# A two-layer diffusion backbone on one core: attention items scored two ahead in two row halves, and the differential head's maps subtracted before they are turned

## The reference

```python
qa,ka,va, qb,kb,vb, cq,ckv,kpe, qd,kd,vd = split(h @ w_in)       # h: norm(x), modulated by adaLN
oa = sdpa(qa, ka, va, sink)                                      # A: windowed, 4 heads, sink logit
ob = rmsnorm(softmax(q1 k1) @ vb - lam * softmax(q2 k2) @ vb)    # B: differential, 4 heads of two maps
oc = sdpa(up(norm(cq)), [up(norm(ckv)), rope(kpe)], v_mla)       # C: latent attention, rank-compressed
od = sdpa(qd, kd, vd, bias)                                      # D: neighbourhood, bias and mask
x += gate * norm(concat(oa, ob, oc, od) @ w_o)
x += gate * norm(ffn(h))      # layer 0: dense SwiGLU; layer 1: top-2 of 8 SwiGLU experts with a router
```

## Time and profile before

| what | us |
|---|---|
| median of 3 runs | 1674.35 (1673.54 to 1676.71) |
| profiled execution | 1674.89 |
| its span, first to last instruction | 1673.1 |
| attention loop, layer 0 (first scores to the first matmul of the projection) | 105.89 to 175.54 |
| the same, layer 1 | 498.01 to 568.65 |
| layer 1, last residual of the mixer to the first gather | 602.85 to 642.0 |
| experts' loop | 642.0 to 1655 |

### The profile page before, as it was taken

One profiled execution on the slowest core, in us unless ns is written; L12 is line 12 of the kernel. 1 busy time (PEld: TensorE's weight loads), 2 busy tenths in 40 slices (PEclk: granted clock), 3 DMA queues, 4 the chain that ended last, 5 costly groups with the idle time before them and its releaser, 6 DMA issues.

```text
span 1673.1 us, 22863 instructions
## 1 busy us (share of the span) xinstructions
PE 1576.5 (94%) x8167; PEld 1295.3 (77%) x8167; DVE 1194.3 (71%) x1014; ACT 976.9 (58%) x958; POOL 89.1 (5%) x142
## 2 busy tenths in 40 slices
PE   5998899999989868999999999999999999999996
PEld 2866789988777747888888888888888888888885
DVE  2556444534556425888888888888888888888885
ACT  4343444434534344776776776776776776776773
POOL 2410040000020010000000000000000000000001
PEclk8999899999989778999999999999999999999998
DMA  9864484577634344998998998998998998998991
GB/s 370 274 195 150 165 257 153 186 240 280 236 117 152 126 152 146 367 368 321 360 371 321 359 369 320 362 365 323 363 363 321 363 365 321 364 365 320 365 366 50
DMA packets 218291, 473.87 MB, mean 283 GB/s; under 512 B 8464, under 2 KB 41536, under 8 KB 218240
## 3 DMA queue, kind: packets, MB, share of 16 engines
q1 hardware_dynamic: 215024, 466.38, 78.3%
q0 software_dynamic: 3216, 6.79, 1.6%
HBM read 470.62 MB, written 2.52 MB: 283 GB/s over the span
## 4 chain that ended last, share of the span: by engine, by line
PE 89%; DVE 4%; ACT 2%; DMA 2%; issue 1%; POOL 1%; POOLq 0%; SPq 0%; DVEq 0%; ACTq 0%
PE ps L1541 22%; PE ps L1546 22%; PE ps L1542 22%; PE ps L1556 3%; PE ps L1557 3%; PE ps L1563 3%; PE ps L1922 2%; PE ps L1751 2%; DMA raw<-in_w_ada 2%; PE ps L1934 1%; PE ps L1715 1%; PE ps L1586 1%; PE ps L1625 1%; DVE w_lo L1060 1%; PE ps L1597 1%
## 5 line engine op out<-in xcount | busy, mean ns | idle before, releaser
L1060 DVE TENSOR_TENSOR w_lo<-raw,w_hi 128x2048 fp32r<-128x2048 f32 (+1 forms) x397 | 903.4, 2284 | 204.7 <-ACT w_hi L712 203.6
L712 ACT ACTIVATE w_hi<-raw 128x2048 fp32r<-128x2048 f32 (+1 forms) x397 | 757.5, 1913 | 254.0 <-PE ps L1542 237.1
L1541 PE MATMUL ps<-w_hi,x_hi 128*128 128x512 f32 (+1 forms) x1216 | 435.2, 370 | 6.5 <-ACT w_hi L712 2.7
L1542 PE MATMUL ps<-w_hi,x_lo 128*128 128x512 f32 (+1 forms) x1216 | 426.7, 363 | 0.0
L1546 PE MATMUL ps<-w_lo,x_hi 128*128 128x512 f32 (+1 forms) x1216 | 284.4, 364 | 0.0
L1541 PEld LDWEIGHTS ps<-w_hi,x_hi 128*128 128x128 f32 x1216 | 228.8, 188 | 47.1 <-issue 7.8
L1542 PEld LDWEIGHTS ps<-w_hi,x_lo 128*128 128x128 f32 x1216 | 228.8, 188 | 36.1
L1546 PEld LDWEIGHTS ps<-w_lo,x_hi 128*128 128x128 f32 x1216 | 206.6, 188 | 39.6
L1541 PE MATMUL ps<-w_hi,h_hi 128*128 128x512 f32 x528 | 207.8, 394 | 0.0
L1542 PE MATMUL ps<-w_hi,h_lo 128*128 128x512 f32 x528 | 207.4, 393 | 0.0
L1546 PE MATMUL ps<-w_lo,h_hi 128*128 128x512 f32 x528 | 141.2, 392 | 0.0
(11 more groups left out here) (242 smaller groups left out, 1213.1 us busy)
## 6 DMA issues: line engine op xcount, KB each, us to landing
raw<-in_moe_w_gate SPq DMA_DIRECT2D x112, 1024.0 KB, 5.2
raw<-in_moe_w_up SPq DMA_DIRECT2D x112, 1024.0 KB, 5.3
raw<-in_moe_w_down SPq DMA_DIRECT2D x112, 1024.0 KB, 5.2
raw<-in_w_ada SPq DMA_DIRECT2D x48, 1024.0 KB, 5.4
raw<-in_w_in SPq DMA_DIRECT2D x20, 960.0 KB, 11.6
raw<-in_ffn_w_gate SPq DMA_DIRECT2D x11, 1024.0 KB, 5.4
raw<-in_ffn_w_up SPq DMA_DIRECT2D x11, 1024.0 KB, 6.4
raw<-in_ffn_w_down SPq DMA_DIRECT2D x11, 1024.0 KB, 5.2
```

Of the source, the lines that this page charges most:

```text
L712: act.activation(split_hi(c, slice(0, width(c))), raw[:, r % NRAW, 0:width(c)], ACT.Copy).then_inc(hi_done, 1)
L1060: dve.tensor_sub(split_lo(c, n), raw[:, raw_of(c) % NRAW, n], split_hi(c, n)).then_inc(lo_done, 1)
L1541: pe.matmul(out, xh, split_hi(c, w), start=start, stop=False, skip_group_check=True)
L1542: last = pe.matmul(out, xl, split_hi(c, w), start=False, stop=False, skip_group_check=True)
```

## The change

Four things change. (1) Items are scored two ahead rather than one; `probs` gets four buffers (on the memory of `x_hi` and `x_lo`, which are free then). (2) For s = 1 the scores use only the 64 rows in which a head's queries aren't zero, alternating between the two halves of the array, which write two PSUM banks; heads of C and D are stored in the order 0, 2, 1, 3. (3) In B0 and B1 DVE's `soft_diff(i + 1)` subtracts the second map, scaled, from the first, so that two maps are turned, copied and multiplied with the values, where there were four. (4) Orders are moved: C5 before C3 and C4; `ada` 20 and 21 into items 8 and 9 (and before the last `w_o` units in the stream); `w_o` units split in items 6, 8 and 9; `out_T` of stream 0 into banks 0 and 1, without its wait for the fifth modulation row; the router's load behind item 9's output; and in layer 1, ACT copies the last modulation row and splits the second expert unit ahead of `norm_sq(1, 1, 1)`.

```diff
-LATER = ["C2", "C3", "C4", "C5"]
+LATER = ["C2", "C5", "C3", "C4"]
...
-        units += ada(l, 12, 13, 14, 15, 16, 17) + wo[:1] + ada(l, 18) + wo[1:2] + ada(l, 19) + wo[2:]
+        units += ada(l, 12, 13, 14, 15, 16, 17) + wo[:1] + ada(l, 18) + wo[1:2] + ada(l, 19, 20, 21) + wo[2:]
...
-        probs = nc.alloc_sbuf_tensor_at("probs", [P, 2, 4, 256], F32, offset=x_hi_at)
+        probs_all = nc.alloc_sbuf_tensor_at("probs", [P, 2, 2, 4, 256], F32, offset=x_hi_at)
...
-            return ps[:, 6:8, :] if s == 0 else ps[:, 4:6, :]
+            return ps[:, 4 * s:4 * s + 2, :]
...
+                if l:
+                    pool.wait_ge(o_evac, 20)
+                    pool.dma_start(rtr, router[0].rearrange("(k p) e -> p k e", p=P)).then_inc(in_rtr, 16)
...
-            pool.wait_ge(x_upd, 6)
-            pool.dma_start(rtr, router[0].rearrange("(k p) e -> p k e", p=P)).then_inc(in_rtr, 16)
...
# ACT, the attention loop
+                for i in range(2):
+                    exps(l, i)
                 for i in range(10):
-                    if i in (4, 8):
-                        rows(l, 2 + i // 4)
-                    exps(l, i)
                     if i in (0, 2, 4, 6):
                         prep(l, len(FIRST[0]) + i // 2)
-                    if i in (6, 8):
-                        split_to(wo_u(l, 0) + i // 2 - 2)
+                    if i + 2 < 10:
+                        exps(l, i + 2)
+                    if i in (3, 7):
+                        rows(l, 3 + i // 4)
+                    if i >= 6:
+                        split_to(wo_u(l, 0) + {6: 1, 7: 1, 8: 2, 9: 3}[i])
...
                 norm_h(l, 1, 0)
                 if l == 0:
                     norm_hi(l, 1, 0)
+                else:
+                    rows(l, 5)
+                    split_to(wo_u(l, 2) + 2)
                 norm_sq(l, 1, 1)
-                if l:
-                    rows(l, 5)
...
# DVE
+            def soft_diff(l, i):
+                s = i % 2
+                nk = nk_of(s)
+                dve.wait_ge(o_evac, 10 * l + i - 1)
+                dve.wait_ge(probs_ready, 10 * l + i + 1)
+                link(dve.reciprocal(sm[:, s, 20:24], sm[:, s, 8:12]))
+                link(dve.scalar_tensor_tensor(out=sm[:, s, 24:26], in0=sm[:, s, 8:12:2], scalar=lam[:, 4:5], in1=sm[:, s, 21:24:2],
+                                              op0=ALU.mult, op1=ALU.mult))
+                for h in range(2):
+                    last = dve.scalar_tensor_tensor(out=probs(i)[:, 2 * h, 0:nk], in0=probs(i)[:, 2 * h + 1, 0:nk],
+                                                    scalar=sm[:, s, 24 + h:25 + h], in1=probs(i)[:, 2 * h, 0:nk],
+                                                    op0=ALU.mult, op1=ALU.add)
+                last.then_inc(diff_ready, 1)
...
                 soft_pre(l, 0)
+                soft_pre(l, 1)
                 for i in range(10):
-                    if i + 1 < 10:
-                        soft_pre(l, i + 1)
                     soft_T(l, i)
+                    if i + 1 < 10 and ITEMS[(i + 1) // 2] in ("B0", "B1"):
+                        soft_diff(l, i + 1)
+                    if i + 2 < 10:
+                        soft_pre(l, i + 2)
                     if i in (1, 3, 5, 7):
                         prep(l, len(FIRST[1]) + i // 2)
...
-                    if i in (6, 8):
-                        split_to(wo_u(l, 0) + i // 2 - 2)
+                    if i >= 6:
+                        split_to(wo_u(l, 0) + {6: 1, 7: 1, 8: 2, 9: 3}[i])
...
# PE
+                def rows(n):
+                    return slice(64 * (n // 2), 64 * (n // 2) + 64) if s else slice(0, P)
+
+                for group in ((0, 2), (1, 3)) if s else ((0,), (1,), (2,), (3,)):
+                    for n in group:
+                        h = head_at(it, n)
+                        m = 2 * (h % 2) + h // 2 if it == "A" else h
+                        k = nk * (KEYS[it] + (h // 2 if it in ("C", "D") else 0))
+                        last = pe.matmul(v[:, n, :], qz[rows(n), QZ[it], s, m, :], keys[s][rows(n), k:k + nk], start=True, stop=it != "C")
...
                 item_scores(l, 0)
+                item_scores(l, 1)
                 for i in range(10):
-                    if i + 1 < 10:
-                        item_scores(l, i + 1)
                     item_T(l, i)
+                    if i + 2 < 10:
+                        item_scores(l, i + 2)
                     if i < 8:
                         prep(l, i % 2, len(FIRST[i % 2]) + i // 2)
-                        ada(l, 12 + i)
+                    ada(l, 12 + i)
...
-                pe.wait_ge(row_evac, SECTIONS.index((l, 4)) + 1)
...
-                ada(l, 20)
+                ada(l, 22)
                 norm_T(l, 1, 0)
-                for n in (21, 22, 23):
-                    ada(l, n)
+                ada(l, 23)
```

More of the change, by code:

```diff
@@ L790, in exps @@
                 for h in range(4):
-                    src = probs[:, s, h, 0:nk] if biased else score_view(s)[:, h, :]
-                    last = act.activation(probs[:, s, h, 0:nk], src, ACT.Exp, bias=sm[:, s, 4 + h:5 + h],
+                    src = probs(i)[:, h, 0:nk] if biased else score_view(s)[:, h, :]
+                    last = act.activation(probs(i)[:, h, 0:nk], src, ACT.Exp, bias=sm[:, s, 4 + h:5 + h],
                                           scale=1.0 if biased else SCALE[it], accum_out=sm[:, s, 8 + h:9 + h])
@@ L1181, in soft_pre @@
                 if it == "D" and s == 1:
-                    pv = probs[:, 1, :, :]
-                    dve.scalar_tensor_tensor(out=pv[:, :, 0:P], in0=v[:, :, 0:P], scalar=sc,
-                                             in1=bm.rearrange("p (h k) -> p h k", h=4), op0=ALU.mult, op1=ALU.add)
+                    pv = probs(i)
+                    for a in range(2):
+                        dve.scalar_tensor_tensor(out=pv[:, 2 * a:2 * a + 2, 0:P], in0=v[:, 2 * a:2 * a + 2, 0:P], scalar=sc,
+                                                 in1=bm.rearrange("p (b a k) -> p a b k", b=2, a=2)[:, a], op0=ALU.mult, op1=ALU.add)
                     link(dve.tensor_scalar(pv[:, :, P:2 * P], v[:, :, P:2 * P], sc, None, ALU.mult))
@@ L1710, in item_scores @@
                 if i >= 8:
-                    pe.wait_ge(prep_evac[s], np_(s) * (l + 1))
-                for h in range(4):
-                    m = 2 * (h % 2) + h // 2 if it == "A" else h
-                    k = nk * (KEYS[it] + (h // 2 if it in ("C", "D") else 0))
-                    last = pe.matmul(v[:, h, :], qz[:, QZ[it], s, m, :], keys[s][:, k:k + nk], start=True, stop=it != "C")
+                    pe.wait_ge(prep_evac[s], np_(s) * (l + 1) - 1)
+                def rows(n):
[6 more added lines that the diff above has]
+                        last = pe.matmul(v[:, n, :], qz[rows(n), QZ[it], s, m, :], keys[s][rows(n), k:k + nk], start=True, stop=it != "C")
                     if it == "C":
                         k = nk * KEYS["rope"]
-                        last = pe.matmul(v[:, h, :], qz[:, QZ["rope"], s, h, :], keys[s][:, k:k + nk], start=False, stop=True)
+                        for n in group:
+                            last = pe.matmul(v[:, n, :], qz[rows(n), QZ["rope"], s, n, :], keys[s][rows(n), k:k + nk], start=False, stop=True)
                 last.then_inc(scores, 1)
@@ L1728, in item_T @@
                 for kb in range(1 + i % 2):
-                    for h in range(4):
-                        last = pe.transpose(ps[:, kb, cols(h, P)], probs[:, i % 2, h, cols(kb, P)], ident())
+                    for h in range(2 if pairs else 4):
+                        last = pe.transpose(ps[:, kb, cols(h, P)], probs(i)[:, 2 * h if pairs else h, cols(kb, P)], ident())
                 last.then_inc(pT, 1)
@@ L1734, in item_out @@
                 it, s = ITEMS[i // 2], i % 2
-                n = 10 * l + i
-                pe.wait_ge(pt_evac, n + 1)
-                if n:
-                    pe.wait_ge(o_evac, n)
-                for h in range(4):
+                if it == "C":
+                    pe.wait_ge(prep_evac[s], np_(s) * (l + 1))
+                pe.wait_ge(pt_evac, 10 * l + i + 1)
+                if l or i:
+                    pe.wait_ge(o_evac, 10 * l + i)
+                for n in range(2 if it in ("B0", "B1") else 4):
+                    h = head_at(it, n)
                     if it == "A":
```

52 lines of the change are left out of this document (31 added, 21 removed).

## The result

The kernel before takes 1673.94 us (median, 1673.44 to 1676.71). The changed kernel takes **1646.45 us** (four runs: 1641.05, 1646.1, 1646.8, 1648.74), a ratio of 0.9828 with a 95% interval of 0.9801 to 0.9854. The forecast of 1641 is 5.5 us low; the time lies in its range, and the change is faster. Its profiled execution is the one of 1641.05, with a span of 1639.2 for 1673.1: 33.9 us less, where the sum of the prediction said 33.2. It is the fastest of the four.

A forecast was written before the change was run, and what follows sets the result against it. The unchanged experts' loop, 1005 of 1673.1 us, passes on whatever is gained ahead of it. Attention's 15.2 plus 18.0 behind layer 1's mixer make 33.2, taking 1674.89 to 1641.7, median 1641; range 1633 to 1655.

The forecast's parts named there:

- The order decides: Attention loops: new order followed queue to queue gives 62.0 for 69.65 us, 7.6 us a layer, 15.2 for both.
- the stretch that was counted as DVE's: Attention loop, from T1's copy to the end of soft_pre(8): DVE has no gap, 26.3 us.
- Row halves: Attention scores of s = 1: 5.0 us a layer off PE; with no overlap the path is 0.7 us a layer longer.
- scores, both halves at once, 0.95: Attention: s = 1 scores take 0.95 us in place of 1.78 with both array halves working at once.
- the prediction's own estimate with ten changes: Attention: ten more tiling changes a layer, up to 0.15 us each, leave 3.5 of the row halves' 5.0 us.
- Halved maps: Attention, B0 and B1: two maps for four halve transposes and outputs, 4.2 us a layer off PE; DVE isn't relieved.
- The tail: Behind layer 1's mixer: earlier router load and ACT's new order start the top-2 choice earlier, 18.0 us gained.
- the gates at full clock: Behind layer 1's mixer: gates take 1.8 us, for 3.58 at half clock, ending at 610.9.
- The prediction's own bound for half clock: Behind layer 1's mixer: with PE at half clock throughout, gates and logits end at 616.6, a gain of 16.8 us.
- I leave the 3.2 in: Attention: old order counted 66.4 for the trace's 69.65; these 3.2 us, mostly PE's half-speed tail, stay in the new count.
- The rival of the kept clock: Attention loops' ends and projection: PE keeps its clock, so the gain is 45 us, 1630; chance 0.07.
- DVE holding everything up: Attention, B items: soft_diff waits for late exponentials with DVE's queue behind it; gain only 21 us, 1653; chance 0.17.

The follow-up runs named there:

- four maps with full rows: Changed kernel with both row halves and subtracted maps undone, scoring two ahead and moved orders kept: 1648.92 us, ratio 0.9845.
- four maps alone: Changed kernel without soft_diff, four maps turned, copied and multiplied again in B0 and B1, row halves kept: 1651.96 us, ratio 0.9863.
- both versions: Changed kernel with 14, 8 and 24 matmuls feeding nothing: 1643.31 us; changed kernel with full rows, 8 and 18 such matmuls, memsets moved: 1638.95 us.
- the filled kernel: Changed kernel plus identity matmuls feeding nothing: 14 after out_T(0) per layer, 8 before stream 1's norm, 24 before the first gather: 1643.31 us.
- the early load with ACT's new order: Kernel before with the early router load, and modulation row and second expert unit ahead of stream 1's sum of squares: 1660.97 us, ratio 0.9921.
- the late load: Changed kernel with the router's load back at its old place: 1658.32 us, ratio 0.989.

## Why the prediction held, point by point

The sum's agreement with the profiled execution (33.9 for 33.2) is in part luck: attention gave 1.9 us more than forecast and the start 1.2 that nobody forecast, the tail 0.9 less, and two stretches between them lost 1.5.

- **The order decides**: right, and shown. Attention fell by 17.1 us for both layers in the profiled execution, where 15.2 were forecast. One item ahead costs 14.0 of it. The wait that it leaves in front of the projection, 3.1 us, came out to the tenth, and the stretch that was counted as DVE's, 26.3 us, as 26.5. That DVE alone holds it isn't borne out: PE is as full there, and more of the last chain is PE's.
- **Row halves**: the step "scores, both halves at once, 0.95" was 0.11 too low (1.06), and it left out what the change of tiles costs outside the scores, 0.2 us an item. Of the 5.0 us a layer, 3.3 come off PE (some 0.48 in four items, 1.33 in C); the prediction's own estimate with ten changes, 3.5, was the nearer one. The halves do overlap: their matmuls start 6 or 7 ns apart (114.347 and 114.354 in the trace). The prediction gave them 0.7 us a layer on the path. The experiment gives nothing or a small loss in the whole kernel, so the 1.4 us of both layers were too much. Why what the traces have in attention doesn't reach the median stays open; the clock's drops lie elsewhere in the two kernels. The Trainium skill (TensorE: Matmul & The Clock Gate, Part 3, Measured speedup vs the span model) has packed matmuls take one's duration and about 4 ns for each further tile; the trace has 6 to 7.
- **Halved maps**: forecast as 4.2 us a layer off PE at a small cost to DVE, with no price of its own on the path. Undone they cost 7.0 us in both layers together: they were needed. Whether by PE's 4.2 us or by the halved copies (418 ns for 685) isn't separated, since both engines are nearly full in that stretch. `soft_diff` isn't free: at 125.2 in layer 0 it stands on the last chain with 1.0 us. But the additive count failed: four maps with full rows was expected dearer than either and is cheaper than four maps alone.
- **The tail**: 18.0 forecast, 17.1 measured from residual to gather, 16.5 from the projection's first matmul. The step that was off is the gates at full clock (1.8 us): they took 3.78. The norm's scale on POOL took 1.28 us for the 0.22 in the rows that the step was read from, so ACT's new order cost 2.1 us of delay where 1.0 was counted. The prediction's own bound for half clock (16.8) was the better value. The load does nearly all of it: 14.3 us alone, 11 to 15 if undone. ACT's new order was argued to free the gates' modulation; alone it shows no gain.
- **"I leave the 3.2 in"**, the correction for half clock. It was right in the mean of the layers, and its spread wasn't seen. Layer 0 came out at 60.33 with 3.9 us of the tail at half clock, layer 1 at 62.87 with 7.8 and, in another execution, 64.2.
- **The median, 5.5 us above the forecast**. The sum was made for one execution and holds for one (33.9 for 33.2). The thirteen executions of the changed kernel go from 1638.37 to 1648.74 at clocks from 0.977 to 0.969, with a correlation of -0.94 between time and clock; those of the kernel before stay within 1671.7 to 1676.7. Within the range, the median's 5.5 us are what the prediction had no term for: it should have given a spread of several executions beside the sum. The traces show two places where executions differ, layer 1's tail (1.4 us) and the stretch from the first gather into the first expert (3.0 us), each with a drop of the clock; that the spread of the rest is of this kind is argued from the correlation. What brings a drop to a place in one run and not in the next stays open.

The rival of the kept clock was true in part: `out_T` ran at full clock in both layers, but each loop kept a stretch at half clock, and so did each projection. Of DVE holding everything up nothing is seen: PE's waits for the maps in layer 0 are 1.7 us for the first exponentials and 1.0 for a copy. The period of an expert didn't move. (The experts' loop, 1005 us in the prediction, is 1013 by the times in the table; nothing hangs on it.)

The parts don't add to the whole. Undone one at a time they cost 14.0 (second item ahead), 11 to 15 (load), 7.0 (maps) and about -2 (row halves), some 32 us for a gain of 27.5 to 31.1. Items ahead and halved maps meet in the same stretch of DVE and PE; that this is why wasn't tested.

## What to carry to other kernels

Follow the new order of the queues step by step before pricing any instruction: a second item in flight was worth 14 us, a load moved by 40 us another 14, and matmuls made 1.6 times as fast nothing that the medians show, although some of them stood on the chain that ended last. Where PE's work is cut beside waits that stay, its clock may take part of the gain (argued here, not shown), so give a forecast the spread of several executions, not of one. A filling with matmuls that feed nothing raised the clock in both versions and ran past its successor's readiness in both; that it pays wasn't shown.

## What the runs showed of the hardware

- **Executions of one program differ by 10 us** (0.6%), in step with the mean granted clock: about 1.3 us for 0.001 of clock in the thirteen of the changed kernel. The kernel before, with the same levels of 1.2 and 2.4 GHz and longer waits, spreads by half of that, and only loosely in step with its clock (0.963 to 0.969, correlation -0.47 over the 21 executions beside the experiments). Nor is it a price list: the filled kernel raised the mean clock by 0.005 and won at most 4 us.
- **A drop at the start of the first expert costs 2 us.** In the six traces with 3.4 us at half clock there (the changed kernel again, both with four maps, the early load with ACT's new order, the late load, the filled kernel) the first expert's first matmul lies 1025.1 to 1025.3 us ahead of the end, in the other eight 1023.1 to 1023.5.
- **Matmuls on the identity hold the clock up**: a mean of 0.969 to 0.977 becomes 0.976 to 0.980, and a gather of 32 records takes 3.74 us in place of 5.54. Not everywhere: in the filled kernel's trace the two attention loops ran at 0.94 and 0.85, below the changed kernel's 0.97 and 0.91.
- **The change of the array's tiling is cheap but not free**: four slots of 0.216 us are 0.86, and the scores take 1.06; another 0.09 us is lost ahead of them and 0.10 between the first two matmuls behind them. So coming and going cost 0.35 to 0.4 us together (items 3, 5, 7 and 9 of both layers). The Trainium skill (TensorEngine Tiling, Tiling Modes, Key Properties) has a change of mode drain the array; the trace fits that and puts this size on it.
- **A small operation on POOL has two durations**: the same addition on 128x1 takes 0.22 to 0.29 us in most places and 1.25 to 1.28 in three of the changed kernel's, at 188.7, 588.0 and 1630.2.
